# Both columns of a chunk in turn behind a norm, three more unread products, and other ticks for attention and the delta rule

## The chip, the core and the metric

One core of a Trainium2 chip runs the kernel. It has five engines with their own instruction streams: TensorE (matrix products and transposes, results in the eight PSUM banks), VectorE, ScalarE, GpSimd and SyncE, which here only issues loads. The metric is the time of one execution on the device in microseconds; less is better.

## The reference

Two transformer blocks in a row over 256 positions of width 1024, in float32. What matters here:

```python
# block 1
h = rms_norm(x, norm_mix_pre); proj = h @ w_in            # stick-breaking attention, convolution, gates
x = x + rms_norm(merged @ w_out, norm_mix_post)
h = rms_norm(x, norm_ffn_pre)
x = x + rms_norm((gelu(g) * a) @ w_down, norm_ffn_post)   # a, g: causal convolution of h @ w_up
# block 2
u = rmsnorm(x, norm_mix_g); proj = u @ w_in_2
o_a = gated_delta_rule_chunked(qh, kh, vh, g, beta)       # chunks of 64, needs inverses of unit triangular blocks
o_b = forgetting_attention(fqh, fkh, fvh, log_f)          # softmax(q k^T * scale + cum_t - cum_s), causal, 8 heads
h = x + (sigmoid(gate_a) * y_a + sigmoid(gate_b) * y_b) @ w_out_2
x = h + square(relu(rmsnorm(h, norm_mlp_g) @ w_up_2)) @ w_down_2
```

## The kernel before

All weights pass through TensorE in 146 *units* of 1 MB or 0.5 MB (`unit_of`, list `units`). SyncE loads a unit into one of three raw buffers. ScalarE copies it, in two halves, to the rounded form `wh` (line 1417). VectorE subtracts that from the raw values and gets the low part `wl` (line 825); for the units in `POOL_HALF`, from U_GK to U_GK + 8 among others, GpSimd does the second half (line 666). Inputs are split in the same way into `xh` and `xl`. Each product of the mathematics is three products on TensorE: xh with wh (j = 0), xl with wh (j = 1), xh with wl (j = 2). A unit of mode "B" has eight chunks of the contraction (q = 0 to 7) and two columns of 128 outputs (c = 0, 1), so 48 products of 256 columns (line 1961). Units of mode "A" have 24 products of 512 columns.

The order of everything else is written by hand in *ticks*: each unit has 8 ticks, six products of 256 columns or three of 512 each. Each engine walks through the same units. Per tick it first advances the steps in `soon` (the splits of the weights two units ahead, the elementwise work behind a unit) and then those in `side` (attention, norms of its queries and keys, delta rule). `pause(n)` lets n ticks pass, `at.to(n)` goes to tick n of a generator. An engine works strictly in the order so given, and stands still in a wait with all that comes behind. Between units ScalarE empties PSUM (`gdn_conv`, line 1622, behind each unit U_GK + v), and VectorE's multiply-adds (line 859) wait for that.

Places that the change touches:

- `norm(n)`: TensorE transposes the normed input into PSUM banks 3 to 6, ScalarE makes the eight chunks of `xh` (line 1465), VectorE those of `xl`. The first unit behind it waits for every chunk: unit 0, U_UP for the second norm, U_UP2 for the last one (`x_of`). With `fresh`, column 0 takes all of j = 0 and 2 first, then all j = 1; column 1 follows. With `by_parts` (U_UP2) the first half of the chunks was there earlier.
- `settle(bank)`: a product of the identity's first 64 rows into a bank that nobody reads afterwards. It stands behind several groups of foreign products already.
- `decays`: four steps r = 0 to 3, each with eight instructions on VectorE (line 1026), an exponential on ScalarE (1576; for r = 2 and 3 eight more, 1572) and a product on GpSimd (719). Ticks from `decays_at(r)`, counted from U_FQ + 6.
- `fox_attention(s)`: heads in pairs (s = 0, 1; i = 0 to 3), 22 ticks for a pair. TensorE makes the scores S, 15 ticks later the transposes of the weights (line 1921, sS), 4 later the outputs (sT). Between them VectorE biases, masks and takes the maxima (1060, 1063, 1066), ScalarE the exponentials (1603), VectorE the reciprocals (1069), ScalarE scales (1608). VectorE's scores of pairs one to four fall in units U_FV + 2, U_GK, U_GK + 3 and U_GK + 6.
- The delta rule (`gdn`, `turned_v`, `chain`, `solve`, `o_turn`), started in tick 6 of U_GK + 8: eight head products (2187, 2188; ticks `head_at`), inverses of 16 x 16 blocks on VectorE between four DMAs, then for c = 0 to 3 three levels (ticks `level_at(c, i)`: transposes of Yt, ScalarE copies, products, VectorE), then `solve`, whose last step sets off the norm of the outputs, then their turning in U_G2 + 1, for the units from U_YG on.

Of the kernel before, what the change touches and what calls it, by code (L numbers as in the profile page):

```python
# [59 lines left out]


def decays_at(r):
    return 4 + 10 * r


class Ticks:
# [26 lines left out]


def level_at(c, i):
    return 73 + 2 * c + 8 * i


def solve_at(g):
    return 104 + 2 * g  # L100


def pause(n):
    for _ in range(n):
        yield


def two_blocks(nc, x, norm_mix_pre, w_in, conv_mix_w, w_att_branch, w_conv_branch, w_out, norm_mix_post,
# [4 lines left out]
    with ctx:  # L113
# [30 lines left out]
        XH = fixed("xh", [P, 8, T], F32R)  # L144
# [673 lines left out]
        def vector(e):  # L818
# [225 lines left out]
            def fox_attention(s):  # L1044
                S, O, sc = PS[3 + s], PS[5 + s], sS[s]
                halves = ((0, 128), (128, 384))
                m0, l0 = (stt2[:, k, 2 * s:2 * s + 2] for k in (6, 7))

                def diag(t):
                    return t[:].rearrange("p (b t) -> p b t", b=3)[:, 0::2, :]  # L1050

                yield from pause(15)
                for i in range(4):
                    h = s + 2 * i
                    yield from pause(2)
                    e.wait_ge(*fox_pe[s]("s", i))
                    e.wait_ge(sums_in, 16)
                    e.wait_ge(*fnp[0]("c", 3))
                    for n, (u, v) in enumerate(halves):
                        e.scalar_tensor_tensor(sc[:, u:v], S[:, u:v], G_D[:, n, h:h + 1], CS[:, h, 0:v - u], ALU.mult, ALU.add  # L1060
                                               ).then_inc(fox_dve[s].sem)
                    e.wait_ge(*fox_dve[s]("b1", i))
                    e.tensor_tensor(diag(sc), diag(sc), diag(MK3), ALU.add).then_inc(fox_dve[s].sem)
                    e.wait_ge(*fox_dve[s]("mask", i))
                    for n, (u, v) in enumerate(halves):
                        e.tensor_reduce(m0[:, n:n + 1], sc[:, u:v], AX, ALU.max, negate=True).then_inc(fox_dve[s].sem)
                    yield from pause(5)
                    e.wait_ge(*fox_act[s]("x1", i))
                    e.reciprocal(l0, l0).then_inc(fox_dve[s].sem)
                    yield from pause(15)  # L1070
                    e.wait_ge(*fox_act[s]("oh", i))
                    e.tensor_tensor(obL[:, h, :], O[:, 0:256], obH[:, h, :].bitcast(F32), ALU.subtract
                                    ).then_inc(fox_dve[s].sem)
# [210 lines left out]
            u = U_DN + 5  # L1284
# [57 lines left out]
            for i in range(4):  # L1342
                unit(U_GZ + i)
            for i in range(4):
                unit(U_G2 + i, 3 if i == 1 else None, lambda: side.add(o_turn()))
            for i in range(4):
                unit(U_YG + i)
                sl = slice(2 * i, 2 * i + 2)
# [56 lines left out]
        def scalar(e):  # L1405
# [186 lines left out]
            def fox_attention(s):  # L1592
                S, O, sc = PS[3 + s], PS[5 + s], sS[s]
                halves = ((0, 128), (128, 384))
                m0, l0 = (stt2[:, k, 2 * s:2 * s + 2] for k in (6, 7))
                me, dv = fox_act[s], fox_dve[s]
                yield from pause(15)
                for i in range(4):
                    h = s + 2 * i
                    yield from pause(2)  # L1600
                    e.wait_ge(*dv("r1", i))
                    for n, (u, v) in enumerate(halves):
                        e.activation(sc[:, u:v], sc[:, u:v], ACT.Exp, bias=m0[:, n:n + 1], accum_out=l0[:, n:n + 1]
                                     ).then_inc(me.sem)
                    yield from pause(5)
                    e.wait_ge(*dv("rec", i))
                    for n, (u, v) in enumerate(halves):
                        e.activation(sc[:, u:v], sc[:, u:v], ACT.Identity, scale=l0[:, n:n + 1]).then_inc(me.sem)
                    yield from pause(9)
                    e.wait_ge(*fox_pe[s]("t", i))  # L1610
                    copy(sT[s][:], S[:, 0:384]).then_inc(me.sem)
                    yield from pause(4)
                    e.wait_ge(*fox_pe[s]("o", i))
                    copy(obH[:, h, :], O[:, 0:256]).then_inc(me.sem)
                    yield from pause(2)
# [258 lines left out]
                unit(U_GZ + i)  # L1874
                gate(U_GZ + i, gz[:, 2 * i:2 * i + 2, :], gzs, ACT.Silu)
            for i in range(4):
                unit(U_G2 + i, 3 if i == 1 else None, lambda: side.add(o_turn()))
                gate(U_G2 + i, sg2[:, 2 * i:2 * i + 2, :], ga2)
            for i in range(4):
                unit(U_YG + i)  # L1880
# [36 lines left out]
        def tensor(e):  # L1917
# [5 lines left out]
            def mul(o, l, r, start=True, stop=True):  # L1923
                return e.matmul(o, l, r, start=start, stop=stop, skip_group_check=True)  # L1924

            def unit(u, xh, xl, x_hi=None, x_lo=None, fresh=False, by_parts=False, at=None, begins=None):


                _, kc, mode, bank, k0, first, done = units[u]
# [4 lines left out]
                passes = [(q, j) for q in range(kc) for j in range(3)]  # L1934
                late = [(q, j) for q in range(kc) for j in (0, 2)] + [(q, 1) for q in range(kc)]
                order = [(c, q, j) for c in range(2) for q, j in (late if fresh and c == 0 else passes)]
                if by_parts:
                    order = [(c, q, j) for c in range(2) for q, j in passes if q < half]
                    order += [(c, q, j) for js in ((0, 2), (1,)) for c in range(2) for q, j in passes if q >= half and j in js]
                ends = [max(n for n, (c, _, _) in enumerate(order) if c == part) for part in range(2)]  # L1940
                begun = set()
                for n, (c, q, j) in enumerate(order):
# [16 lines left out]
                    cs = slice(c * P, (c + 1) * P)  # L1959
                    l, r = (W[:, cs], X) if mode == "B" else (X[:, cs], W)  # L1960
                    k = e.matmul(o, l, r, start=opens, stop=done and n == ends[c], skip_group_check=True)  # L1961
                    begun.add(use if by_parts else (use, c))
                    if n == ends[c]:
                        k.then_inc(mm.sem)
                    if n % every == every - 1:
# [79 lines left out]

            def x_of(n):
                r = 8 * turn_of(n)
                return dict(x_hi=lambda q: xth("hi", r + q), x_lo=lambda q: xtl("lo", r + q), fresh=n < 3, by_parts=n == 3)


            def rest_of_gains():
# [113 lines left out]
            def gdn():  # L2165
# [13 lines left out]
                for h in range(NH):  # L2179
# [5 lines left out]
                    if h >= 2:  # L2185
                        e.wait_ge(*gat("y", h - 2))
                    e.matmul(PS[3 + h % 3][:], gkq[:, h, 0, 0:P], gkq[:, h].rearrange("p k t -> p (k t)"), start=True, stop=True)
                    e.matmul(PS[6 + h % 2][:, 0:T].rearrange("p (k t) -> p k t", k=2), gkq[:, h, 0, P:T], gkq[:, h, :, P:T], start=True,
                             stop=True).then_inc(gkk.sem)

            def turned_v(c):
                a, g = c // 2, c % 2
                at = Ticks()
                yield from at.to(turn_v_at(c))
                e.wait_ge(*gsl("v"))
                e.wait_ge(*gat("y", NH - 1))
                for j in range(4):
                    k = turn(PS[3 + c][:, j * P:(j + 1) * P], gv[:, 4 * g + j, a * P:(a + 1) * P])
                k.then_inc(ch_pe[c].sem)

            def chain(c):
                a, g = c // 2, c % 2
# [136 lines left out]
                unit(U_GB + 2 * i, XH, XL)  # L2339
                unit(U_GB + 2 * i + 1, obH, obL, lambda q: fox_act[q % 2]("oh", q // 2), lambda q: fox_dve[q % 2]("ol", q // 2))  # L2340
            for u in range(U_GZ, U_YG):
                unit(u, XH, XL, at=3 if u == U_G2 + 1 else None, begins=lambda: side.add(o_turn()))
            for i in range(4):
                unit(U_YG + i, oaH, oaL, lambda q: oth("hi", q // 2), lambda q: otd("lo", q // 2))
            for i in range(4):
# [2 lines left out]
                    side.add(out2_turned(i // 2))  # L2348
            for i in range(FC2 // 2):
                unit(U_UP2 + i, XH, XL, **(x_of(3) if i == 0 else {}))  # L2350
            for u in range(U_DN2, NU):
                unit(u, f2H, f2L, lambda q: u2a("h", q // 2), lambda q: u2d("lo", q // 2))

# [29 lines left out]
```

## Time and profile before

| | us |
|---|---|
| median of three runs | 911.55 (910.73 to 911.75) |
| the profiled execution, its own time | 912.79 |
| its span | 911.1 |
| TensorE busy | 893.4 |
| VectorE busy | 573.4 |
| ScalarE busy | 498.5 |
| GpSimd busy | 135.4 |

All times of the trace are microseconds from the start of the span. The profile was taken on one execution, whose own time is 1.7 us over its span. PE is TensorE, DVE VectorE, ACT ScalarE, POOL GpSimd. Products overlap in the records: each of 256 columns lasts 0.28 us, but the next starts long before its end, so the pace is read from starts, or from the count in a stretch.

### The profile page before, as it was taken

Reading aid. Unit: us, or ns where it says so; the run is one execution under the profiler, and the core shown is the slowest. Engines: PE = TensorE matmul, PEld = TensorE weight load, DVE = VectorE, ACT = ScalarE, POOL = GpSimd, SP = SyncE. Lnnn points to the kernel's source line nnn. Section 1 sums busy time; section 2 is a strip of 40 time slices with the busy share of each in tenths; the row PEclk is TensorE's granted clock in tenths of the full one; section 3 lists DMA queues with packets and bytes.
Section 4 is the critical chain, followed back from the end, with each engine's and each line's share of the span. In section 5 each row is a group of like instructions: output and inputs, shape, how many; then the busy total and the mean of one; then the engine's idle time right before and its main releaser. Section 6 shows DMA issues by size and latency. Waiting matters only on the chain.

```text
span 911.1 us, 15622 instructions
## 1 busy us (share of the span) xinstructions
PE 893.4 (98%) x6445; PEld 827.0 (91%) x6445; DVE 573.4 (63%) x824; ACT 498.5 (55%) x771; POOL 135.4 (15%) x151
## 2 busy tenths in 40 slices
PE   8999999999999999999998999999999999999998
PEld 7899999889999988788798988999999899998886
DVE  4556554768887845667667797765376665554442
ACT  5576864556556634556774764333554565554330
POOL 6011101511111100133343110000010012110000
PEclk9999999999999999999999999999999999999999
DMA  8743264675654657356444445532246646665560
GB/s 283 261 156 117 94 231 160 211 216 181 202 191 164 192 202 256 113 163 254 140 140 141 144 138 176 160 113 74 94 140 216 193 148 199 203 200 189 185 204 23
DMA packets 132594, 156.33 MB, mean 172 GB/s; under 512 B 9353, under 2 KB 106028, under 8 KB 132268
## 3 DMA queue, kind: packets, MB, share of 16 engines
q1 hardware_dynamic: 125844, 151.78, 51.3%
q10 hardware_dynamic: 6680, 3.56, 1.3%
q8 instruction: 51, 0.84, 0.4%
q14 instruction: 19, 0.16, 0.0%
HBM read 153.08 MB, written 2.24 MB: 170 GB/s over the span
## 4 chain that ended last, share of the span: by engine, by line
PE 79%; DVE 11%; ACT 4%; DMA 3%; issue 2%; POOL 1%; SPq 0%; ACTq 0%; POOLq 0%
PE ps L1961 67%; PE ps L1924 3%; PE ps L1992 3%; DVE wl L825 2%; PE ps L2211 2%; PE ps L1921 2%; DVE gkq L859 2%; DVE gv L859 1%; ACT wh L1417 1%; DMA U<-blocks 1%; DMA raw<-in_w_in 1%; DMA Yc<-inverses 1%; DMA blocks<-last 1%; DVE mt L1258 1%; DVE sS L1060 1%
## 5 line engine op out<-in xcount | busy, mean ns | idle before, releaser
L825 DVE TENSOR_TENSOR wl<-raw,wh 128x1024 fp32r<-128x1024 f32 (+1 forms) x275 | 327.3, 1208 | 192.4 <-ACT wh L1417 192.3
L1961 PE MATMUL ps<-xh,wh 128*128 128x256 f32 x1280 | 362.4, 284 | 0.9 <-ACT xh L1465 0.9
L1961 PE MATMUL ps<-xh,wl 128*128 128x256 f32 x1280 | 354.2, 277 | 0.4 <-POOL wl L666 0.4
L1961 PE MATMUL ps<-xl,wh 128*128 128x256 f32 x1280 | 351.0, 277 | 0.0
L1417 ACT ACTIVATE wh<-raw 128x1024 fp32r<-128x1024 f32 (+1 forms) x292 | 286.7, 1024 | 110.8 <-PE ps L1961 89.6
L1961 PEld LDWEIGHTS ps<-xh,wh 128*128 128x128 f32 x1280 | 241.2, 188 | 4.6 <-issue 1.4
L1961 PEld LDWEIGHTS ps<-xh,wl 128*128 128x128 f32 x1280 | 240.6, 188 | 0.6 <-POOL wl L666 0.6
L1961 PEld LDWEIGHTS ps<-xl,wh 128*128 128x128 f32 x1280 | 239.5, 188 | 0.3
L666 POOL TENSOR_TENSOR wl<-raw,wh 128x1024 fp32r<-128x1024 f32 (+1 forms) x17 | 43.4, 2555 | 84.5 <-ACT wh L1417 84.2
L1961 PE MATMUL ps<-wh,f2L 128*128 128x512 f32 x128 | 49.8, 389 | 0.0
L1961 PE MATMUL ps<-wh,f2H 128*128 128x512 f32 x128 | 49.8, 389 | 0.0
L1961 PE MATMUL ps<-wl,f2H 128*128 128x512 f32 x128 | 49.8, 389 | 0.0
L811 POOL TENSOR_TENSOR rr<-rr 128x512 f32<-128x512 f32 x16 | 16.7, 1043 | 139.1 <-ACT f2H L1912 139.1
L1961 PE MATMUL ps<-wh,xh 128*128 128x512 f32 x88 | 35.7, 405 | 0.0
L1961 PE MATMUL ps<-wl,xh 128*128 128x512 f32 x88 | 34.5, 392 | 0.0
L1961 PE MATMUL ps<-wh,xl 128*128 128x512 f32 x88 | 34.5, 392 | 0.0
L710 POOL TENSOR_TENSOR ya<-ya,yg 128x512 f32<-128x512 f32 x11 | 16.6, 1509 | 113.1 <-ACT yg L1517 113.1
L859 DVE SCALAR_TENSOR_TENSOR gkq<-ps,cols,gkq 128x255 f32<-128x255 f32 (+2 forms) x48 | 23.0, 480 | 13.4 <-ACT gkq L1622 12.2
L859 DVE SCALAR_TENSOR_TENSOR ya<-ps,cols,ya 128x255 f32<-128x255 f32 (+1 forms) x44 | 21.1, 481 | 15.6 <-ACT ya L1791 14.9
L1961 PEld LDWEIGHTS ps<-wl,f2H 128*128 128x128 f32 x128 | 24.0, 188 | 5.0
L1961 PEld LDWEIGHTS ps<-wh,f2L 128*128 128x128 f32 x128 | 24.0, 188 | 5.0
L1961 PEld LDWEIGHTS ps<-wh,f2H 128*128 128x128 f32 x128 | 24.0, 188 | 4.9
(324 smaller groups left out, 1381.0 us busy)
## 6 DMA issues: line engine op xcount, KB each, us to landing
raw<-in_w_in SPq DMA_DIRECT2D x55, 1024.0 KB, 5.0
raw<-in_w_up SPq DMA_DIRECT2D x38, 1024.0 KB, 5.2
raw<-in_w_down SPq DMA_DIRECT2D x26, 1024.0 KB, 5.0
raw<-in_w_out SPq DMA_DIRECT2D x8, 1024.0 KB, 5.0
raw<-in_w_proj_fox SPq DMA_DIRECT2D x4, 1024.0 KB, 5.1
raw<-in_w_proj_gdn SPq DMA_DIRECT2D x4, 1024.0 KB, 4.9
raw<-in_w_conv_branch SPq DMA_DIRECT2D x4, 512.0 KB, 3.3
raw<-in_w_att_branch SPq DMA_DIRECT2D x4, 512.0 KB, 3.3
```

The costliest lines, as they stand in the source:

```text
L666: signals(e.tensor_tensor(L, R, H.bitcast(F32), ALU.subtract), lop)
L710: signals(e.tensor_tensor(ya[s][:], ya[s][:], yg[s][:], ALU.mult), fpr)
L811: signals(e.tensor_tensor(r[:], r[:], r[:], ALU.mult), u2p)
L825: e.tensor_tensor(L, R, H.bitcast(F32), ALU.subtract).then_inc(lo.sem)
L859: return e.scalar_tensor_tensor(o, i, s, acc, ALU.mult, ALU.add)
L1060: e.scalar_tensor_tensor(sc[:, u:v], S[:, u:v], G_D[:, n, h:h + 1], CS[:, h, 0:v - u], ALU.mult, ALU.add).then_inc(fox_dve[s].sem)
L1417: e.activation(tile_of(WH, u)[:, k:kc, :], tile_of(RAW, u)[:, k:kc, :], ACT.Copy).then_inc(hi.sem)
L1921: return e.transpose(o, i, ident[:])
L1924: return e.matmul(o, l, r, start=start, stop=stop, skip_group_check=True)
L1961: k = e.matmul(o, l, r, start=opens, stop=done and n == ends[c], skip_group_check=True)
L1992: k = e.matmul(main_ps(u, a), X, W, start=first and n == 0, stop=done and ends, skip_group_check=True)
L2211: k = e.matmul(o[j], l[j], r[j], start=True, stop=True)
```

## The change

The first units behind a norm take both columns of a chunk in turn: for each chunk that is not known yet j = 0 and j = 2 of both columns, then all of j = 1. Unit 0 leaves j = 2 of the second half of its chunks until all of j = 0 is done. Three more unread products stand behind the last head product of the delta rule (one tick later, after a wait for a head's result on VectorE), behind the last transposes of its values, and behind the first unit of U_UP2. In attention, VectorE takes the scores one tick earlier (the reciprocals stay), and ScalarE the exponentials two ticks later (the scaling stays). The decay steps r = 1 and 2 come three and six ticks earlier on all engines that do them, r = 0 and 3 stay. The levels, the solve and the turning of the outputs come two ticks later.

```diff
 def decays_at(r):
-    return 4 + 10 * r
+    return 4 + 7 * r + 9 * (r == 3)
 def level_at(c, i):
-    return 73 + 2 * c + 8 * i
+    return 75 + 2 * c + 8 * i
 def solve_at(g):
-    return 104 + 2 * g
+    return 106 + 2 * g
 # VectorE, fox_attention
-                    yield from pause(2)
+                    yield
                     e.wait_ge(*fox_pe[s]("s", i))
...
-                    yield from pause(5)
+                    yield from pause(6)
                     e.wait_ge(*fox_act[s]("x1", i))
                     e.reciprocal(l0, l0).then_inc(fox_dve[s].sem)
 # ScalarE, fox_attention
-                    yield from pause(2)
+                    yield from pause(4)
                     e.wait_ge(*dv("r1", i))
...
-                    yield from pause(5)
+                    yield from pause(3)
                     e.wait_ge(*dv("rec", i))
 # VectorE, ScalarE and TensorE, the turned outputs
-                unit(U_G2 + i, 3 if i == 1 else None, lambda: side.add(o_turn()))
+                unit(U_G2 + i, 5 if i == 1 else None, lambda: side.add(o_turn()))
 # TensorE, unit
-                if by_parts:
-                    order = [(c, q, j) for c in range(2) for q, j in passes if q < half]
-                    order += [(c, q, j) for js in ((0, 2), (1,)) for c in range(2) for q, j in passes if q >= half and j in js]
+                if from_norm:
+                    known = [q for q in range(kc) if by_parts and q < half]
+                    order = [(c, q, j) for c in range(2) for q, j in passes if q in known]
+                    later = [q for q in range(kc) if u == 0 and q >= half]
+                    for q in range(kc):
+                        if q not in known:
+                            order += [(c, q, j) for j in ((0,) if q in later else (0, 2)) for c in range(2)]
+                    order += [(c, q, 2) for q in later for c in range(2)]
+                    order += [(c, q, 1) for q in range(kc) if q not in known for c in range(2)]
...
-                return dict(x_hi=lambda q: xth("hi", r + q), x_lo=lambda q: xtl("lo", r + q), fresh=n < 3, by_parts=n == 3)
+                return dict(x_hi=lambda q: xth("hi", r + q), x_lo=lambda q: xtl("lo", r + q), from_norm=True, by_parts=n == 3)
 # TensorE, gdn, behind the head products
+                yield
+                e.wait_ge(*gat("x", 5))
+                settle(5)
 # TensorE, turned_v
                 k.then_inc(ch_pe[c].sem)
+                if c == 3:
+                    settle(7)
 # TensorE, U_UP2
                 unit(U_UP2 + i, XH, XL, **(x_of(3) if i == 0 else {}))
+                if i == 0:
+                    settle(7)
```

## Rows read from the trace of the kernel before

**Rows 1.** The page: busy time of the engines; the chain that ended last.

```profile
PE 893.4 (98%) x6445; PEld 827.0 (91%) x6445; DVE 573.4 (63%) x824; ACT 498.5 (55%) x771; POOL 135.4 (15%) x151
...
PE 79%; DVE 11%; ACT 4%; DMA 3%; issue 2%; POOL 1%; SPq 0%; ACTq 0%; POOLq 0%
```

**Rows 2.** Waits of TensorE: who waited for whom, sum, times, longest.

```profile
PE ps L1921 <- ACT sS L1608: 2.7, 1, 2.7
```

**Rows 3.** TensorE by stretch: length, busy (records), granted clock, DMA share, GB/s.

```profile
10.16:16.90 6.74, 6.34 (x48) 1.00 0.62 205
189.99:196.58 6.59, 6.59 (x48) 1.00 0.95 272
...
461.50:471.50 10.00, 10.00 (x90) 1.00 0.38 121
...
490.40:493.30 2.90, 0.23 (x3) 0.91 0.00 0
493.30:496.30 3.00, 3.00 (x14) 0.52 0.64 174
...
558.00:572.00 14.00, 14.00 (x121) 1.00 0.92 272
...
590.00:604.00 14.00, 13.92 (x123) 1.00 0.54 169
...
745.00:759.00 14.00, 14.00 (x126) 1.00 0.66 202
```

**Rows 4.** Timeline at unit 0: start, length, engine, line, operation, [idle before <-releaser].

```profile
9.55 3.01 ACT L1465 ACTIVATE xh<-ps,cols 128x256 fp32r<-128x256 f32 x8
...
12.37 0.38 PE L1961 MATMUL ps<-xh,wl 128*128 128x256 f32 x1 [0.40 <-POOL wl L666]
```

**Rows 5.** Timeline of TensorE: an unread product (two records) and what follows.

```profile
460.85 0.49 PE L1924 MATMUL ps<-ident 64*128 64x128 f32 x2
461.27 0.38 PE L1961 MATMUL ps<-xh,wh 128*128 128x256 f32 x1
```

**Rows 6.** Timeline around the first attention pair.

```profile
432.86 2.01 ACT L1417 ACTIVATE wh<-raw 128x1024 fp32r<-128x1024 f32 x2 [2.02 <-PE ps L1961]
...
437.17 0.60 PE L1921 MATMUL ps<-ident,fkm 128*128 128x128 f32 x4
...
439.33 0.67 ACT L1590 ACTIVATE fqm<-ps,cols 128x512 f32<-128x512 f32 x1
...
440.06 1.58 PE L1924 MATMUL ps<-fqm,xs 128*128 128x128 f32 x8 [0.89 <-ACT fqm L1590]
...
443.38 1.86 DVE L1063 TENSOR_TENSOR sS<-sS,mk 128x256 f32<-128x256 f32 x1
```

**Rows 7.** Timeline around the second and third attention pair.

```profile
462.18 0.40 ACT L1603 ACTIVATE sS<-sS,stt 128x128 f32<-128x128 f32 x1 [3.25 <-DVE stt L1066]
...
465.55 2.00 ACT L1417 ACTIVATE wh<-raw 128x1024 fp32r<-128x1024 f32 x2
465.68 1.52 DVE L859 SCALAR_TENSOR_TENSOR gkq<-ps,cols,gkq 128x255 f32<-128x255 f32 x3 [1.78 <-ACT gkq L1622]
467.12 1.22 DVE L825 TENSOR_TENSOR wl<-raw,wh 128x1024 fp32r<-128x1024 f32 x1
...
469.87 1.50 ACT L1608 ACTIVATE sS<-sS,stt 128x128 f32<-128x128 f32 x4 [2.32 <-DVE stt L1069]
...
477.44 2.37 POOL L666 TENSOR_TENSOR wl<-raw,wh 128x1024 fp32r<-128x1024 f32 x1 [0.42 <-ACT wh L1417]
477.54 3.35 DVE L825 TENSOR_TENSOR wl<-raw,wh 128x1024 fp32r<-128x1024 f32 x1
...
492.44 1.49 ACT L1608 ACTIVATE sS<-sS,stt 128x128 f32<-128x128 f32 x4 [2.32 <-DVE stt L1069]
```

**Rows 8.** Timeline at the first block transposes of the delta rule.

```profile
589.24 1.89 DVE L1133 TENSOR_TENSOR Yt<-Yc,m 128x512 f32<-128x512 f32 x3 [3.09 <-DMA Yc<-inverses]
...
590.08 0.63 PE L1921 MATMUL ps<-ident,Yt 128*128 128x128 f32 x4 [1.83 <-DVE Yt L1133]
```

More of the change, by code:

```diff
@@ L1876, in scalar @@
             for i in range(4):
-                unit(U_G2 + i, 3 if i == 1 else None, lambda: side.add(o_turn()))
+                unit(U_G2 + i, 5 if i == 1 else None, lambda: side.add(o_turn()))
                 gate(U_G2 + i, sg2[:, 2 * i:2 * i + 2, :], ga2)
@@ L1924, in mul, with unit @@
                 return e.matmul(o, l, r, start=start, stop=stop, skip_group_check=True)
-            def unit(u, xh, xl, x_hi=None, x_lo=None, fresh=False, by_parts=False, at=None, begins=None):
+            def unit(u, xh, xl, x_hi=None, x_lo=None, fresh=False, by_parts=False, from_norm=False, at=None, begins=None):
                 _, kc, mode, bank, k0, first, done = units[u]
@@ L1936, in unit @@
                 order = [(c, q, j) for c in range(2) for q, j in (late if fresh and c == 0 else passes)]
-                if by_parts:
-                    order = [(c, q, j) for c in range(2) for q, j in passes if q < half]
-                    order += [(c, q, j) for js in ((0, 2), (1,)) for c in range(2) for q, j in passes if q >= half and j in js]
+                if from_norm:
[7 more added lines that the diff above has]
+                    order += [(c, q, 1) for q in range(kc) if q not in known for c in range(2)]
+                assert sorted(order) == sorted((c, q, j) for c in range(2) for q, j in passes)
                 ends = [max(n for n, (c, _, _) in enumerate(order) if c == part) for part in range(2)]
@@ L1961, in unit @@
                     k = e.matmul(o, l, r, start=opens, stop=done and n == ends[c], skip_group_check=True)
-                    begun.add(use if by_parts else (use, c))
+                    begun.add(use if from_norm else (use, c))
                     if n == ends[c]:
@@ L2341, in tensor @@
             for u in range(U_GZ, U_YG):
-                unit(u, XH, XL, at=3 if u == U_G2 + 1 else None, begins=lambda: side.add(o_turn()))
+                unit(u, XH, XL, at=5 if u == U_G2 + 1 else None, begins=lambda: side.add(o_turn()))
             for i in range(4):
```

## The prediction

> **What bounds the kernel now.** I read the head of the page first. TensorE is busy for 893.4 of 911.1 us, and 79% of the chain that ended last is TensorE's own; VectorE has 11%, ScalarE 4% [rows 1]. So the kernel is a stream of products, and a change can gain only in two ways: products that start sooner after one another, or moments in which TensorE stands still. The list of waits of TensorE and the timeline around each give the second kind. Three lie in what the change touches: 2.7 us once for the transposes of attention weights [rows 2], 1.83 us for the block inverses of the delta rule [rows 8], 0.89 us for a norm of the keys [rows 6]. The first kind is read from the table of stretches. An undisturbed stretch of 256-column products (745 to 759 us) holds 126 records; (14.00 + 0.28) / 126 is one product per 113.3 ns, the 0.28 being the last product's own length. From 558 to 572 us there are 121, so 118.0 ns: a second, slower pace at the same granted clock of 1.00. The first units behind a norm are slower still: 48 products take 6.74 us at 10.16 and 6.59 us at 189.99. And from 493.3 to 496.3 us the granted clock is 0.52, that is, near the lower level of 1.2 GHz, directly after the 2.90 us from 490.4 in which TensorE did almost nothing [rows 3]. That is the dearest spot: a stall, and behind it half speed.
>
> **First units behind a norm.** ScalarE makes the eight chunks of the normed input in 3.01 us, one each 0.36 to 0.38 us [rows 4]. In the old order column 0 alone takes two products of a chunk (0.23 us) and then waits for the next chunk. In the new order both columns take it, four products or 0.45 us, so TensorE becomes the slower of the two and is not held after the first chunk. 48 products at 113.3 ns are 5.44 us; I add 0.2 for the first chunks. Unit 0: 6.74 - 5.64 = 1.1 us. It includes the 0.40 us wait for GpSimd's low half [rows 4]: the change puts the eight high products of chunks 4 to 7 (0.9 us) ahead of the low ones, and by then (about 12.9 us) that half, which came at 12.37, is there. First feed-forward unit: 6.59 - 5.64 = 0.95 us. What comes after is not held by these: ScalarE and VectorE split unit 1 straight behind the chunks, from 12.6 us on, two steps of 1.0 and two of 1.2 us [rows 7], partly side by side, done by 16.5; TensorE asks for its second half near 17.4. Last norm (unit U_UP2): here 24 of the 48 products ran already; of the next eight, two to a chunk, three pairs come 0.13 us late each (0.36 against 0.23), so 0.4 us.
>
> **Three more unread products.** The nearest rows are the pair that one such product leaves in attention: 0.42 us from 460.85 to 461.27 [rows 5]. TensorE is a little late at a change of shape, so I take 0.5 us each, bounds 0.4 and 0.6. What it can give is the fast pace: from 461.5 us, behind the attention pair, 90 records stand in 10 us [rows 3], (10.00 + 0.28) / 90 = 114 ns. It pays from 0.5 / 0.0047 = 106 products on. Behind the last head product there are about 130 slow ones until the turned values (gain 0.6), behind the turned values 78, then 90 (gain 0.4). Both places lie before a stall (next part), so gain and loss, -0.1 and +0.1, vanish in it: 0, and 1.0 if that cover is gone and no pace is won. Behind the first unit of U_UP2 the pace is fast already (the 126 records from 745 us), so there it costs 0.5. With the 0.4 from above that place nets +0.1 us. It would pay 3.3 us if the new order alone led into the slow pace (700 x 4.7 ns); I don't see a reason for that.
> The Trainium skill, TensorEngine Tiling (Array Packing), Key Properties, says that changing the tiling mode drains TensorE. Read so, each of the three is a loss of its own, 1.5 us in all against my 0.5. The pair's 0.42 us agrees that the change of rows costs; that the products behind it keep the fast pace is what the rule does not tell.
>
> **Decays (ticks of r = 1 and 2 earlier).** Today VectorE's and ScalarE's part of r = 2 sits right before the first attention pair: ScalarE runs its eight exponentials and one more, keeps a half of v, and only then does the last key norm at 439.33 to 440.0; TensorE, which had turned its keys at 437.17, waits 0.89 us and starts at 440.06 [rows 6]. All instructions of r = 2, on VectorE, ScalarE and GpSimd, move six ticks ahead, those of r = 1 three; none issues a DMA. ScalarE stood idle for 2.02 us up to 432.86 [rows 6], and takes the 2.5 us there, at a cost of 1.1 us to its next copies, which has room. Then the key norm follows its transposes at once (437.8 to 438.4), before TensorE's arrival at 439.0. Gain 440.06 - 439.0 = 1.05 us. VectorE reads the same row table for r = 0 already, so no load is waited for. What is late next is ScalarE up to the first transposes at 452.4; its work there moves with it.
>
> **Attention ticks.** In program order, VectorE's scores move one tick and ScalarE's exponentials two. For the first, third and fourth pair nothing on ScalarE lies between the old and the new place, and on VectorE only the first pair moves (ahead of one low half). For the second pair the exponentials cross the end of unit U_GK: today ScalarE waits in front of them, does them from 462.18 to 464.8, and only then empties PSUM of U_GK (0.8 us) and splits the next weights (465.55, 2.00 us) [rows 7]. TensorE had ended that unit near 462.7 (twelve products behind 461.27 [rows 5]). In the new order ScalarE does the emptying and the splitting in the time in which it waited (463.0 to 465.7), the exponentials until 467.7, and VectorE, free at 463.9 and no longer waiting for the emptied unit until 465.68, reaches its reciprocals at 467.95, not 469.7. The weights are scaled 1.7 us sooner than at 469.87. This runs on: the next unit is emptied 1.7 us sooner too, and VectorE comes to its low half at 476.95 instead of 477.54. There today GpSimd starts its own at 477.44, and VectorE's takes 3.35 us where the one at 467.12 took 1.22: it stood still until GpSimd's 2.37 us were over [rows 7]. Starting half a microsecond ahead of GpSimd it escapes, and 0.6 + 2.1 = 2.7 us come off the third pair, of which 2.55 arrive (ScalarE's own steps). Its scaling, now 492.44, comes at 489.9; the transposes can start at 490.75 instead of 493.30. TensorE gets there at 490.46. Left are 0.3 us for the first head and about as much for the second, 0.65. Today it loses 2.84 us there, and in the 3.0 us from 493.3 only 14 records stand, some 1.5 us of products at the full clock: 1.45 more lost at the half. Behind the 1.83 us wait of rows 8 the clock stays at 1.00 [rows 3], so a wait of 0.65 should not lower it. Gain 2.84 + 1.45 - 0.65 = 3.6 us. The fourth pair is served as today: its times hang on TensorE.
> The Trainium skill, SBUF — State Buffer, section on its two separate sides, states an exclusive lock between the two engines: whichever starts first has it for its whole instruction. The 3.35 us agree. By that rule the half microsecond decides everything at 477 us, which is the first rival.
>
> **Delta rule two ticks later, turned outputs too.** The first transposes wait from 588.1 to 590.08 us. Their input is at 589.24 on VectorE, straight behind a load [rows 8], at the end of a row of DMAs that does not move. Two ticks later TensorE has done twelve more products in that wait, 12 x 113 to 118 ns = 1.35 us, and the 2.0 us shrink to some 0.6. All later levels, the solve and the turned outputs keep their distances; their slots in a unit are the old ones shifted by one chain, and from the turning of the outputs to U_YG there are 19 ticks instead of 21, for work that is spread over twelve. Gain 1.35 us, bounds 0 and 2.0.
>
> **Sum** against the profiled execution: 912.79 us (span 911.1 and 1.7 around it). 1.1 + 0.95 - 0.1 + 1.05 + 3.6 + 1.35 = 7.95, so 904.85. It stands 1.24 above the median of 911.55; the median then is 903.6.
>
> **Rivals.**
> (a) The third pair's stall stays. If VectorE loses the race at 477 us it is 2.1 us late, the wait is 2.7 or so and the clock falls again: the 3.6 us are not gained, 907.2. For it: the margin is 0.5 us, and everything before has moved by other amounts. Against it: GpSimd's start hangs on the same ScalarE copies.
> (b) The unread products are a plain loss: the delta rule's wait is smaller than I think and no pace is won, 1.0 us more: 904.6. Or the shift of the delta rule is given back behind VectorE's order: 1.35, 905.0.
> (c) The first pair's gain is taken back by VectorE: its moved scores meet GpSimd's low half, as the masking at 443.38 us does already with 1.86 us [rows 6]; 1.1 us, 904.7.
> (d) Slower than before: exponentials two ticks (1.4 us) later reach the transposes of pairs two to four undiminished. It decides when ScalarE has no idle time to put the copies in. Then pair two waits 1.2, pair three 4.3, pair four 1.4, outputs as much again, and the clock falls at three places instead of one: 3.6 not gained, + 4.0 + 2.9 + 3: 917. Against it: ScalarE's 3.25 us wait before 462.18 [rows 7].
> (e) Nothing left at the third pair and in the delta rule: 1.2 less, 902.4.
>
> **How the numbers follow.** Forecast 903.6 (0.58); (a) 0.20; (b) 0.09; (c) 0.05; (d) 0.04; (e) 0.04. The range takes in (b), (c), (e), and (a) with another 1 us: 902.2 to 908.3. Measurement can tell 0.2%, 1.8 us: same is 909.7 to 913.4. Faster 0.94, same 0.02, slower 0.04.
>
> **What would show it.** In the trace after: 48 products of the first two such units in 5.6 to 5.7 us; the first attention pair directly behind its unit's last product; VectorE's low half near 477 (some 3 us earlier by then) at 1.2 us and not 3.3; no stretch with a granted clock under 0.9; some 0.6 us left before the first block transposes; 126 and not 121 records in 14 us behind the head products. Wrong would be: a wait over 2 us at any pair, a clock drop, 121 records behind an unread product.

## The result: 6.7 us less, and the profile after

The changed kernel takes 904.9 us (median; 904.5 to 905.0) where the kernel before, on the same chip, takes 911.6: a ratio of 0.9926, 95% interval 0.9914 to 0.9938. Its profiled execution took 904.9 us too. The head of the page, against [rows 1]:

```profile
span 903.2 us, 15634 instructions
...
PE 892.1 (99%) x6451; PEld 826.8 (92%) x6451; DVE 572.7 (63%) x824; ACT 498.2 (55%) x771; POOL 136.0 (15%) x151
...
PE 88%; DVE 6%; ACT 3%; issue 1%; DMA 1%; POOL 1%; SPq 0%; POOLq 0%; ACTq 0%
```

TensorE's work is the same to 1.3 us; the span is 7.9 us shorter. VectorE's share of the chain that ended last fell from 11% to 6%. The list of TensorE's waits (who waited for whom, us, times, longest), whose line before was [rows 2]:

```profile
PE ps L1921 <- DVE xs L868: 2.4, 2, 1.7
PE ps L1924 <- POOL ident L609: 1.6, 1, 1.6
PE ps L2000 <- DVE wl L825: 0.9, 1, 0.9
PE ps L1924 <- POOL at L695: 0.7, 1, 0.7
PE ps L1924 <- ACT sT L1449: 0.6, 1, 0.6
```

The 2.7 us for the attention weights are gone, and so are the waits for the key norm and for the block inverses. TensorE by stretch (columns as in [rows 3]; the first two lines, the fourth and the fifth answer lines there):

```profile
10.04:15.75 5.71, 5.71 (x48) 1.00 0.75 249
189.09:194.71 5.62, 5.62 (x49) 1.00 0.99 267
195.12:309.48 114.36, 114.36 (x1009) 1.00 0.59 196
487.08:490.08 3.00, 2.86 (x26) 1.00 0.64 179
550.68:564.68 14.00, 14.00 (x124) 1.00 0.93 266
572.21:582.90 10.69, 10.69 (x91) 1.00 0.72 189
727.66:730.57 2.91, 2.91 (x24) 1.00 0.00 1
730.99:812.71 81.72, 81.72 (x721) 1.00 0.61 194
```

At the third pair (487.08) there are 26 records in 3 us at a clock of 1.00, where before there were 14 at 0.52. In this document the first pace is that of 113.3 ns a product and the second that of 117.8 ns, both at a granted clock of 1.00. Behind the heads it is now the first: 124 records, and starts 113.3 ns apart. Behind the turned values the products still run at the second pace: 10.69 us for 91 records is 117.5 ns, although an unread product stands right in front of them. The timeline at the places of [rows 6 to 8]:

```profile
434.86 0.67 ACT L1590 ACTIVATE fqm<-ps,cols 128x512 f32<-128x512 f32 x1
...
437.01 1.47 PE L1924 MATMUL ps<-fqm,xs 128*128 128x128 f32 x8
...
473.41 1.21 DVE L825 TENSOR_TENSOR wl<-raw,wh 128x1024 fp32r<-128x1024 f32 x1
...
473.91 2.93 POOL L666 TENSOR_TENSOR wl<-raw,wh 128x1024 fp32r<-128x1024 f32 x1 [2.09 <-ACT wh L1417]
...
486.19 1.49 ACT L1608 ACTIVATE sS<-sS,stt 128x128 f32<-128x128 f32 x4 [2.31 <-DVE stt L1069]
...
583.20 0.63 PE L1921 MATMUL ps<-ident,Yt 128*128 128x128 f32 x4
```

VectorE now starts its low half 0.5 us ahead of GpSimd, and it takes 1.21 us, not 3.35; GpSimd's own takes 2.93, not 2.37. The scaling at 486.19 comes 6.25 us earlier than the one at 492.44.

Lining up the two traces at TensorE's groups gives where the 7.9 us went, each number being the growth of the distance between the same group before and after: start 0.1; unit 0 0.8; first feed-forward unit 1.0; up to the first attention pair 1.2, of it 1.07 at the key norm's wait; the first pair's transposes 0.35; third pair 3.9; between the turned values and the block solves 1.0; the second up projection -0.3. The rest is under 0.1 each.

### The profile page after: what moved, and what is told of

Its sections match the earlier page's. It is cut to its first block, busy times and chain, and to the rows that moved or that the text cites. A ratio compares the mean times of both kernels' runs of the same rounds, so it can differ in the third digit from the quotient of the medians.

```text
span 903.2 us, 15634 instructions
## 1 busy us (share of the span) xinstructions
PE 892.1 (99%) x6451; PEld 826.8 (92%) x6451; DVE 572.7 (63%) x824; ACT 498.2 (55%) x771; POOL 136.0 (15%) x151
## 4 chain that ended last, share of the span: by engine, by line
PE 88%; DVE 6%; ACT 3%; issue 1%; DMA 1%; POOL 1%; SPq 0%; POOLq 0%; ACTq 0%
PE ps L1969 75%; PE ps L1924 4%; PE ps L2000 3%; PE ps L2224 2%; PE ps L1921 2%; DVE wl L825 1%; DVE gkq L859 1%; DVE gv L859 1%; DMA raw<-in_w_in 1%; PE ps L2195 1%; DVE mt L1258 1%; ACT wh L1417 1%; ACT gkq L1622 0%; ACT sS L1608 0%; PE ps L2107 0%
## 5 line engine op out<-in xcount | busy, mean ns | idle before, releaser
L1969 PE MATMUL ps<-xh,wh 128*128 128x256 f32 x1280 | 357.9, 283 | 0.6 <-ACT xh L1465 0.4
L1969 PE MATMUL ps<-xh,wl 128*128 128x256 f32 x1280 | 350.4, 277 | 0.0
```

## Experiments

Eleven kernels ran, and the changed one a second time, on three chips; every one was compared with the kernel before on its own chip.

### The four parts, each alone

First each group of edits by itself on the kernel before. `order_only`: the new order of products and nothing else:

```
-                return dict(x_hi=lambda q: xth("hi", r + q), x_lo=lambda q: xtl("lo", r + q), fresh=n < 3, by_parts=n == 3)
+                return dict(x_hi=lambda q: xth("hi", r + q), x_lo=lambda q: xtl("lo", r + q), from_norm=True, by_parts=n == 3)
```

with what `from_norm` does in `unit`.

> The kernel before with the new order of products behind the norms alone (first unit, first FFN unit, first unit of the second up projection). Theory A, each part of the change pays by itself what the trace after shows at its place: 0.8 us at the first unit, 1.0 us at the first FFN unit, 0.1 us at the last one, 1.9 us in all, 911.6 to 909.7 us. Rival B, the new order leads TensorE into the slow pace (117.8 instead of 113.4 ns a product) wherever no unread product stands behind it: the 744 products of the second up projection then take 3.3 us more, 913.0 us, and the trace shows them at 117.8 ns. The first group's 102 products should be at 117.8 ns by both.

Measured: 909.4 us (908.0 to 909.6), ratio 0.9934 (0.9916 to 0.9952). Theory A. The second up projection ran at the first pace; the new order doesn't lead into the second one.

`attention_ticks`: the decays, and the attention's pauses on VectorE and ScalarE.

```
-    return 4 + 10 * r
+    return 4 + 7 * r + 9 * (r == 3)
...
-                    yield from pause(2)
+                    yield
...
-                    yield from pause(5)
+                    yield from pause(6)
...
-                    yield from pause(2)
+                    yield from pause(4)
...
-                    yield from pause(5)
+                    yield from pause(3)
```

> The kernel before with the decays' and the attention's ticks alone. Theory A, independent parts: 1.1 us at the first attention pair, some 0.3 us behind it and 3.9 us at the third pair, 5.3 us in all, 906.3 us; no stretch at a granted clock below 0.9 near 494 us. Rival B, the third pair's stall went away because the other parts had shifted the work against the weights' arrival: it is there again without them, 910.2 us, with a wait of over 2 us at the row sums of the third pair.

Measured: 905.8, 906.6, 907.4, 910.6, 910.8 and 910.9 us; ratio 0.9929 (0.9906 to 0.9952). No wait at the third pair and no fall of the clock, so theory A for the mechanism. But what were the two groups of times, four microseconds apart? The profiled execution was one of the second group, 910.6 us. TensorE by stretch, the 1008 products of the first up projection; of `attention_ticks`:

```profile
197.90:316.73 118.83, 118.83 (x1010) 1.00 0.56 184
```

and of the kernel before:

```profile
197.00:311.36 114.36, 114.36 (x1009) 1.00 0.59 193
```

The same instructions in the same order, the same clock of 1.00, yet 117.9 ns a product in one and 113.4 in the other: 4.5 us. The pace of that stretch isn't a property of the instructions but of the execution. The 23 runs of the kernel before on this chip lay between 910.2 and 917.3 us, median 915.3.

`delta_ticks`: the levels and the solve two ticks later, and the turned outputs on three engines.

```
-    return 73 + 2 * c + 8 * i
+    return 75 + 2 * c + 8 * i
...
-    return 104 + 2 * g
+    return 106 + 2 * g
...
-                unit(u, XH, XL, at=3 if u == U_G2 + 1 else None, begins=lambda: side.add(o_turn()))
+                unit(u, XH, XL, at=5 if u == U_G2 + 1 else None, begins=lambda: side.add(o_turn()))
```

> The kernel before with the delta rule's solve and the turned outputs two ticks later, alone. Theory A: of the 2.0 us that TensorE waits for the first blocks, 1.7 us go and nothing comes in their place, 909.9 us. Rival B: the chain that makes the blocks, not the tick, sets the time; the wait stays near 2 us at a later place and the time is 911.6 us.

Measured: 914.4 us median (910.7 to 916.9), ratio 0.9985 (0.9966 to 1.0004): from the times no gain can be told. In its trace the wait for the first blocks is gone and twelve more products stand ahead of it, as theory A has it; the stretch of 1008 took 118.82 us in this execution, so its one time says nothing.

`unread_three`: the three added calls.

```
+                yield
+                e.wait_ge(*gat("x", 5))
+                settle(5)
...
+                if c == 3:
+                    settle(7)
...
+                if i == 0:
+                    settle(7)
```

> The kernel before with the three more unread products of 64 rows alone. Theory A, they cost 0.4 us behind the heads, 0.6 us behind the turned values and 0.4 us in the second up projection; the first two are absorbed by the wait of 2.0 us for the first blocks that follows, and the products between heads and turned values change from 117.8 to 113.4 ns, which that wait absorbs too: 912.0 us. Rival B, they bring the fast pace where it was slow and pay: 911.0 us or below. Rival C, nothing absorbs them: 913.0 us.

Measured: 917.3 us median (912.1 to 919.0), ratio 1.0015 (0.9996 to 1.0033). Lowest, highest and median all lie 1.7 to 2.0 us above those of the kernel before. The interval just takes in no change, but none of the three expectations had that much.

### The changed kernel again

> The changed kernel as it is, once more, beside the kernel before, which in the last call ran between 910.2 and 917.3 us. Theory A, it was the new order behind the norm that made the 1008 products of the first up projection run at 113.3 ns each time (order_only stayed between 908.0 and 909.6 us, while the three kernels with the old order reached 910.9 to 919.0): all its runs lie between 904.4 and 905.5 us, whatever before does. Rival B, the pace of that stretch is open in the changed kernel too: its times fall into two groups, near 904.9 and near 909.4 us.

Measured: 905.2 us (904.7 to 905.7) beside 910.0 to 917.9 for the kernel before; ratio 0.9925 (0.9905 to 0.9945). Theory A. All that have the new order in the first feed-forward unit agree: eight kernels ran 64 times with it, none of these times stands some 4.5 us above the others of its kernel, and their nine traces have 113.4 ns on the 1008 products. Of five traces with the old order there two have 117.9. Which unit does it?

```
- from_norm=True, by_parts=n == 3
+ fresh=n < 3, from_norm=n == 0, by_parts=n == 3
```

> The kernel before with the new order in the first unit alone; the first FFN unit keeps the old order. Theory A, the order of the first FFN unit decides at which pace the 1008 products behind it run: with the old order there the times are spread as those of before are, 0.8 us lower: from some 909.5 to 916.5 us. Rival B, it is the first unit (all later stretches inherit from it): the times stay together, 909.4 to 911.0 us.

Measured: 910.6 us median (908.4 to 916.0), ratio 0.9990 (0.9974 to 1.0006). Eleven times lie between 908.4 and 912.8, one at 916.0. The one is what theory A wants, but it wants more of them. By the times the first feed-forward unit is the likelier cause, no more. The traces add where the pace is fixed: before the long stretch begins. These are the first and the last of the last 18 products of the first feed-forward unit, in the kernel before and in `attention_ticks`:

```profile
194.45 0.28 PE L1961 MATMUL ps<-xh,wh 128*128 128x256 f32 x1
...
196.37 0.28 PE L1961 MATMUL ps<-xh,wl 128*128 128x256 f32 x1
```

```profile
195.28 0.28 PE L1961 MATMUL ps<-xh,wh 128*128 128x256 f32 x1
...
197.28 0.28 PE L1961 MATMUL ps<-xh,wl 128*128 128x256 f32 x1
```

That is 1.92 us and 2.00 us for the same 17 steps, 113 and 117.6 ns each. In all 14 traces the 1008 products kept the pace at which this unit ended: `attention_ticks` and `delta_ticks` have the second pace in both, the other twelve the first. With the new order the unit ended at the first pace nine times out of nine, with the old one three times out of five. Why the old order leaves the pace open stays open.

### What an unread product costs

`no_unread_up2` is the changed kernel less this:

```
                unit(U_UP2 + i, XH, XL, **(x_of(3) if i == 0 else {}))
-                if i == 0:
-                    settle(7)
```

> The changed kernel without the unread product in the second up projection. Theory A, the pace there is fast without it (it was in before and in order_only), so the product is plain cost: 0.4 us less than the changed kernel, 904.5 us. Rival B, the new order leads into the slow pace there: 720 products times 4.4 ns is 3.2 us, less 0.4: 2.8 us more, 907.7 us, and the trace shows 117.8 ns for them.

Measured: 904.5 us (904.2 to 904.9), 0.65 below `after_again` on the same chip. Theory A in the mechanism, with a larger price. The stretch from the last norm to the down projection, of `no_unread_up2`:

```profile
727.89:812.31 84.42, 84.42 (x745) 1.00 0.60 188
```

and of the kernel before:

```profile
735.83:820.60 84.77, 84.77 (x744) 1.00 0.60 187
```

In the changed kernel it is 812.71 - 727.66 = 85.05 us. So the new order gains 0.35 and the unread product costs 0.63. Its own 0.42 is only the middle of it: the product in front of it takes 0.20 us instead of 0.11, and the one behind it 0.22 instead of 0.11. The Trainium skill, TensorEngine Tiling (Array Packing), Key Properties, has TensorE drained at a change of tiling mode; the trace agrees in that going to 64 rows and back costs 0.63 us, part of it in the neighbours. A drain as such it does not show.

`no_unread_delta` leaves out the other two, behind the heads and behind the turned values:

```
-                yield
-                e.wait_ge(*gat("x", 5))
-                settle(5)
...
-                if c == 3:
-                    settle(7)
```

> The changed kernel without the unread products behind the heads and behind the turned values. Theory A, TensorE waits for the first blocks all the same: they are ready at a time that the heads set, so what TensorE saves it waits, and the wait grows from 0.28 to some 0.9 us or more; the time stays at 904.9 us. Rival B, the wait doesn't grow, both are plain cost, 1.0 us less, 903.9 us. Rival C, without them the products between heads and blocks are slow, 222 times 4.4 ns, 1.0 us more, less 1.0 us: 904.9 us too, but with the wait at 0.3 us.

Measured: 903.9 us (903.5 to 904.2), 1.25 below `after_again`. Rival B, and my theory A was wrong: the blocks' time is not fixed behind the heads. VectorE's masking of the loaded inverses, in the changed kernel:

```profile
582.36 1.90 DVE L1133 TENSOR_TENSOR Yt<-Yc,m 128x512 f32<-128x512 f32 x3 [3.02 <-DMA Yc<-inverses]
```

in the same kernel once more (`after_again`):

```profile
580.06 1.90 DVE L1133 TENSOR_TENSOR Yt<-Yc,m 128x512 f32<-128x512 f32 x3 [1.28 <-DMA Yc<-inverses]
```

and in `no_unread_up2`, which is the same up to here, with what TensorE did:

```profile
582.67 1.90 DVE L1133 TENSOR_TENSOR Yt<-Yc,m 128x512 f32<-128x512 f32 x3 [3.34 <-DMA Yc<-inverses]
...
583.51 0.63 PE L1921 MATMUL ps<-ident,Yt 128*128 128x128 f32 x4 [0.82 <-DVE Yt L1133]
```

The inverses go out to memory and come back by two DMAs, and together with the masking's start that took 9.4, 7.6 and 9.8 us from the first issue (572.98, 572.42 and 572.91). Beyond one product's 0.11 us TensorE stands still for 0.28, 0 and 1.0 us. The load's landing beside the weights' moves by 2 us from execution to execution, and the wait for the blocks with it.

What did the two bring in pace? Over the 14 traces, the 132 to 138 products behind the heads ran at 113.3 ns in three of the seven with an unread product in front, and in four of the seven without; the products behind the turned values in five of seven with it and four of seven without. No gain can be seen in these counts. Yet the products are not without effect. In the seven traces without them the pace behind the turned values is the one that stood behind the heads, seven times out of seven (three slow, four fast). In the seven with both it changed six times: four times from slow to fast, twice, `after` among them, from fast to slow. So they switch the pace rather than settle it.

`no_unread` is the changed kernel less the lines of both diffs above, without all three:

> The changed kernel without its three new unread products. Theory A, all three are plain cost and add up: 0.6 us (no_unread_up2) and 1.2 us (no_unread_delta) below the changed kernel's 905.1: 903.4 us, with all runs within 1.2 us and no stretch of 700 or more products at 117.8 ns. Rival B, TensorE saves them only in executions in which the inverses' load lands early; in the others the wait for the first blocks takes it back, and the median is 904.3 us. Rival C, with none of them left the pace of a long stretch is open again: some runs 3 to 4.5 us above the others.

Measured: 903.0 us (902.8 to 904.0), ratio 0.9892 (0.9864 to 0.9921). Theory A. It is 1.9 to 2.1 us below the two medians of the changed kernel (on other chips; the two experiments above, compared with it on one chip, add up to 1.9, and three times 0.63 is 1.9) and the fastest kernel of this study. TensorE's stretches in it:

```profile
195.42:309.78 114.36, 114.36 (x1009) 1.00 0.59 195
551.00:565.00 14.00, 14.00 (x126) 1.00 0.91 269
```

### The third pair: what held VectorE, and what the stall costs

`old_attention` is the changed kernel with the pauses of before, first VectorE's, then ScalarE's:

```
-                    yield
+                    yield from pause(2)
-                    yield from pause(6)
+                    yield from pause(5)
...
-                    yield from pause(4)
+                    yield from pause(2)
-                    yield from pause(3)
+                    yield from pause(5)
```

> The changed kernel with the attention's ticks as before (VectorE's scores and reciprocals, ScalarE's exponentials), all else as changed. Theory A, VectorE's low half of the unit at the third pair starts 0.1 us behind GpSimd's again and takes 3.3 us, TensorE waits 2.9 us at the third pair, and behind it the clock falls in most executions: 2.6 us more than the changed kernel in the runs with a granted clock of 1.000 (907.7), 3.9 us more in those below (909.0). Rival B, the half microsecond of room that I read was won by the decays and the new order: VectorE starts first here too, its half takes 1.2 us, and the time stays near 905.5 us.

Measured: 910.2 us median (908.4 to 911.4), ratio 0.9973 (0.9957 to 0.9989). Theory A. Timeline, then TensorE by stretch:

```profile
474.95 2.37 POOL L666 TENSOR_TENSOR wl<-raw,wh 128x1024 fp32r<-128x1024 f32 x1 [0.41 <-ACT wh L1417]
...
475.05 3.35 DVE L825 TENSOR_TENSOR wl<-raw,wh 128x1024 fp32r<-128x1024 f32 x1
...
490.81 1.59 PE L1921 MATMUL ps<-ident,sS 128*128 128x128 f32 x6 [2.67 <-ACT sS L1608]
```

```profile
487.86:490.81 2.95, 0.28 (x3) 0.91 0.00 0
490.81:493.81 3.00, 3.00 (x14) 0.52 0.66 182
```

All six traces with the old ticks and GpSimd's half have VectorE 0.10 to 0.11 us behind GpSimd here and 3.34 to 3.35 us long. So it is not chance; it comes from the order of each engine's own work behind the same ScalarE copies. Lined up with the changed kernel, the third pair costs 2.8 us at the wait and 1.1 behind it at the low clock. Another 0.7 us, which I had not foreseen, is lost at the first pair: the first head's transposes come 0.33 us later and the second's another 0.37.

That GpSimd is what holds VectorE was still inferred from two rows side by side. So GpSimd's half of unit 83 went to VectorE:

```
-POOL_HALF = frozenset([0, *range(26, 33), *range(78, 87)])
+POOL_HALF = frozenset([0, *range(26, 33), *range(78, 83), *range(84, 87)])
```

> old_attention, and GpSimd has no half of the low part of unit 83 any more (the one it starts at 477.44 us in the kernel before); VectorE makes both halves. Theory A, it is GpSimd's operation that holds VectorE's: the 3.34 us turn into two operations of 1.2 us, the third pair's wait shrinks from 2.9 to 2.0 us, and the time is 0.9 us below old_attention's. Rival B, VectorE's 3.34 us have another reason (its input, the memory): the operation stays long and another one of 1.2 us comes on top; the wait grows to 4.1 us, 1.2 us above old_attention.

Measured: 908.7 us median (907.7 to 909.9), ratio 0.9948 (0.9929 to 0.9966). VectorE's two halves and TensorE's wait:

```profile
475.06 1.21 DVE L825 TENSOR_TENSOR wl<-raw,wh 128x1024 fp32r<-128x1024 f32 x1
...
478.28 1.21 DVE L825 TENSOR_TENSOR wl<-raw,wh 128x1024 fp32r<-128x1024 f32 x1
...
489.82 1.24 PE L1921 MATMUL ps<-ident,sS 128*128 128x128 f32 x6 [1.67 <-ACT sS L1608]
```

The trace has theory A to the digit: same start, 1.21 us instead of 3.35, and the wait a microsecond shorter although VectorE has one more operation. The Trainium skill, SBUF — State Buffer, SBUF: two separate sides, says that a VectorE operation with two inputs in SBUF and a GpSimd operation that reads SBUF exclude each other for a whole instruction; the trace agrees: 0.10 us too late costs 2.14 us.

Now the clock. With a wait of 1.96 us it fell in this execution too. The full clock that is missing is the same, 0.09 x 2.95 + 0.48 x 3.00 = 1.7 us in `old_attention` and 0.24 x 3.00 + 0.33 x 3.00 = 1.7 us here, but here none of it falls into the wait:

```profile
487.86:489.82 1.96, 0.29 (x3) 1.00 0.00 0
489.82:492.82 3.00, 2.85 (x17) 0.76 0.66 187
492.82:495.82 3.00, 3.00 (x18) 0.67 0.46 163
```

while in `delta_ticks` it did not fall behind the full wait:

```profile
495.29:498.24 2.95, 0.28 (x4) 1.00 0.00 0
498.24:501.24 3.00, 2.85 (x23) 1.00 0.64 191
```

So the stall makes the fall possible and does not fix it. The mean granted clock of each run tells which had it: two of `old_attention`'s twelve are at 1.000, and they are its lowest, 908.4 and 908.5 us, against 909.7 to 911.4 for the others. Of `old_attention_half83`'s twelve it is six, at 907.7 to 908.0 (one of them 0.999) against 909.5 to 909.9. By the medians of these groups the fall costs 1.9 us in the first kernel and 1.8 us in the second. The shorter stall had it less often, 6 of 12 against 10 of 12, which is too few to call a rate. Without the fall `old_attention_half83` is 0.6 us below `old_attention`, with it 0.7, where I had expected 0.9; the rest of the 1.5 us between the medians is the count of falls.

### The decays

`old_decays` is the changed kernel with

```
-    return 4 + 7 * r + 9 * (r == 3)
+    return 4 + 10 * r
```

> The changed kernel with the decays at their old ticks, all else as changed. Theory A, the wait of 0.9 us before the first attention pair is back and nothing behind it absorbs it: 1.1 us more than the changed kernel, 906.2 us. Rival B, the order at the third pair hangs on it (VectorE comes a little later against GpSimd, which is not moved by the same amount): the half of 3.3 us is back too, 908.8 us or more. Rival C, later slack takes it back: 905.2 us.

Measured: 906.8 us (905.8 to 907.8), ratio 0.9931 (0.9904 to 0.9957). Theory A, at the place exactly:

```profile
438.68 0.49 PE L1924 MATMUL ps<-fqm,xs 128*128 128x128 f32 x2 [0.88 <-ACT fqm L1590]
```

The distance to the changed kernel grows by 1.08 us there and is not given back before the heads; the third pair has its half of 1.2 us. The median is 1.6 to 1.9 us higher, on another chip. Against the trace of `after_again` 0.5 us more is lost early, at 90 products from 23 us and 42 from 74 us, which ran at the second pace in this execution; whether that is so in the others no trace tells.

## Why the prediction was right where it was, and 1.3 us short

**Units behind a norm.** 1.1 forecast at unit 0, and 6.74 - 5.71 = 1.03 measured; but the 54 products behind it in the same stretch, 6.23 us before, took 6.48, so 0.8 was left. The pace is again that of the execution: of the ten traces with the new order in unit 0, six have these 102 products at the second pace and four at the first. First feed-forward unit: 0.95 forecast, 6.59 - 5.62 = 0.97. U_UP2: 0.4 forecast, 0.35.

**Three unread products.** The term that was mis-sized: I took 0.5 us each, paid once, and the other two made free by the pace they bring and by the wait behind them. The price is 0.63, they switch the pace instead of making it fast, and the cover isn't reliable. The step that failed is the choice of row: the 0.42 us between the pair and its follower leave out the product in front and the one behind. Forecast -0.1 with the order's 0.4, so -0.5 of their own; by the trials -1.9. The first half of rival (b) was this one, at 1.0 us instead of the 1.4 that it is. My sign of being wrong, the second pace behind an unread product, did come, behind the turned values. That the new order leads into the second pace was rightly doubted.

**Decays.** 1.05 forecast, 1.07 measured, and in the place named.

**Attention ticks.** The mechanism was right down to the half microsecond: VectorE ahead of GpSimd by 0.50, its half at 1.21, no stretch under 0.9. Of the forecast 3.6, 3.9 came, since 0.3 us less was left over. The 0.35 at the first pair was missing. What I couldn't know from one trace: the clock's part of it, 1.45 in the sum, is there only in the executions in which the clock falls.

**Delta rule.** The wait went from 1.83 to nothing listed (0.28 of the steps' own), and about 1.7 came at that place instead of 1.35. But the wait was long in that execution of the kernel before. In the five traces with the old ticks the gap at the first blocks, beyond one product, is 2.0, 1.25, 0.75, 0.46 and 0 us (the last is `unread_three`, with two unread products ahead of it): 0.9 on average. A shift that fills it can't give 1.35 each time.

**The anchor.** Taken together the terms were 7.95 against 7.9 in the spans, and that they agree so well is luck. The unread products took 1.4 us more than forecast and unit 0 gave 0.3 less; the third pair gave 0.3 more, the first pair 0.35, the blocks' wait 0.35, and the products behind the heads 0.6, because they happened to run at the first pace in this execution. And still the median gained 6.7, not 7.95: the step that failed is subtracting the whole sum from the median. I had noted that the profiled execution stood 1.24 above it and carried that over as if both kernels had it. The changed kernel's profile was at its median. The excess lay in the profiled execution of before. Where in it is not shown, as the four other times on that chip have no trace. Likely places are the wait for the blocks, 1.1 above its average in the traces, which I then took off in full, and the products behind the heads at the second pace, 0.6 us.

**Rivals.** (a), the third pair's stall stays, did not happen: GpSimd's half came 3.53 us earlier than before (477.44 to 473.91) and VectorE's 4.13 (477.54 to 473.41), so the order of the two turned; `old_attention` shows that it is the attention's ticks that turn it. (c) and (d) did not happen. (e) came about halfway: 0.3 us were left at the third pair and 0.28 in the delta rule, for 0.65 and 0.6 in my sum. None of my cases had the change's second effect, that it makes the times of this kernel narrow: 1.2 us from lowest to highest over ten runs, against 8 for the kernel before. Where the kernel before had 915.3 us as its median, the change would be worth some 10 us by these numbers; it was not measured beside it there.

## What to carry to other kernels

Before a sum of stalls is taken off a median, find out which of them are the same in every execution. Here the wait that hung on the order of another engine's work was (2.67 us in six traces of six); the one behind a DMA's landing (0 to 2.0 us) and the loss at the low clock were not, and their size in one profile is a draw. An operation added only to change an engine's pace is to be priced from the last undisturbed instruction ahead of it to the first one behind it, and taken out again on trial. When VectorE takes three times as long for an operation as for its twins, look whether GpSimd started a tenth of a microsecond ahead, and move one of the two.

## What the runs showed of the hardware that was not expected

- One stretch of 1008 identical 256-column products took 114.36 us or 118.8 us at the same granted clock of 1.00 in different executions of the same instruction order. The pace is kept over the whole stretch, and in all 14 traces it is the pace at which the unit in front had ended; an unread product of 64 rows in between changed nothing there. Elsewhere, behind the turned values, the pace changed in six of seven traces with unread products and in none of seven without. What sets it is open.
- Going to a 64-row product and back costs 0.63 us, a third of it in the products beside it.
- After the same 2.95 us with next to no work TensorE's granted clock fell to 0.52 in one execution and stayed at 1.00 in another; after 1.96 us it fell in half of the executions (6 of 12, by their mean clock).
- VectorE's 1.21 us operation took 3.35 us when it started 0.10 us behind GpSimd's 2.37 us one, and 1.21 us when it started 0.5 us ahead, where GpSimd's then took 2.93.
- A store and a load of 128 KB each through memory, beside the weights' stream, took between 7.0 and 9.8 us until VectorE could use them.
